# Projection of the merged sum: one fp32 product or three fp32r products

## The chip, the cores and the metric

One Trainium2 chip, of which the kernel uses one core. Its engines run side by side: PE (TensorE, matrix products, its results go to the PSUM banks), DVE (VectorE), ACT (ScalarE), POOL (GpSimd) and SP (SyncE), which here issues nearly all transfers from HBM. The metric is the device time of one execution in microseconds (us); lower is better.

## The reference, cut to what matters

The program is a chain of two transformer-like blocks over 256 tokens of width 1024: gated linear attention, product-key retrieval, sliding-window attention, retrieval again, then a mixer of retention and latent attention, and a routed mixture of experts. Everything is in fp32. The change is in the mixer's last two lines:

```python
def token_mixer(...):
    ...
    y_ret = (jax.nn.silu(rg) * y_ret) @ w_ret_o
    y_mla = mla(...) @ w_mla_o
    merged = jax.nn.sigmoid(gate_ret) * y_ret + jax.nn.sigmoid(gate_mla) * y_mla
    return merged @ w_out            # (256, 1024) @ (1024, 1024)
...
h = h + g1 * token_mixer(...)
u = modulate_2(rmsnorm_2(h, norm2[l]), sh2, sc2)
h = h + g2 * hier_moe(u, ...)        # router, top 2 of 32 experts, three products each
```

## The kernel before, in words

Activations are kept with features on the partitions: a tensor of width 1024 is eight chunks of 128 features by T = 256 tokens. A projection makes one output chunk at a time, in one of four PSUM banks that are used in turn. Its weights come as slots of 128 x 1024 values (512 KB) through a ring of four slots (`ring`). SP issues the load of a slot when PE has begun the chunk three before it (`ring_free`).

There are two ways to make a product of an input and a slot. `project` (L871) multiplies in fp32: eight products of 128x128 by 128x256 for a chunk, each recorded as two instructions. `project_split` (L814) splits both operands into a high part, rounded to fp32r, and a low part, the rest, and adds three fp32r products (high by high, high by low, low by high): 24 instructions for a chunk. For that the weights of a slot are split in two halves of 512 columns. ACT writes the high part (`split_high`, L1529: it waits for the slot's landing, and for `x_passed`, by which PE tells that it has begun the half three before, so that one of the four buffers `w_parts` is free). DVE writes the low part by a subtraction (`split_lows`, L2026) and signals `x_low`, for which PE waits. The list `SPLIT` (L91) names the slots that go this way and numbers their halves. The inputs' parts lie in `h_parts`.

Around the change the order is this. PE runs the eight chunks of `mla_o` (tiles `m_out0` to `m_out7`) split. ACT makes the high parts two chunks ahead, DVE the low parts. When a chunk is full, DVE multiplies it by the gate `M.gm` into SBUF (L2674), adds `M.gr` (L2676) and signals `merged`. Then PE runs the eight chunks of `mix_out` (tiles `mix0` to `mix7`) in fp32 from `M.mg` (`project_norm`, L1330). Behind each, DVE adds the result into the residual `xT` (`update_dve`, L2034), ACT squares it (`squares_act`, L1512), and from the third chunk on PE adds up a chunk of squares with a matrix of ones (L770). After chunks 3 and 5, ACT also makes high parts of the first expert's weights (`experts_high`), and POOL their low parts (`moe_pool`, L2899, four instructions at L2903).

Then comes the root of the norm: ACT writes a logarithm and an exponential of the sum of squares, DVE the mean (L1951) and three steps of refinement in `root_dve` (L1959, L1961, L1963), then eight scalings (L1976) that ACT shifts (L1576). Meanwhile PE multiplies five times by the unit matrix for nothing (`keep_clock`, L866), and then begins the router's product (L1352), each step of which waits for a shifted chunk. The routing and the experts follow.

SP's queue there: the loads of `mix_out` 0 to 3, then, once `merged` is 1, two of 1 MB for the first expert (L707), then `mix_out` 4 to 7 and the router.

Of the kernel before, what the change touches and what calls it, by code (L numbers as in the profile page):

```python
# [39 lines left out]
P = 128  # L40
D = 1024
T = 256
# [51 lines left out]
          ("gate_r", 0, 8), ("gate_m", 0, 8), ("mla_o", 0, 8)) for k in range(first, last)]  # L94
# [116 lines left out]
def block_program(nc, stream, vecs, xin, pos, wg2, subk, consts, consts_g, consts_s, consts2, consts_e, out):  # L211
    ctx = ExitStack()
    with ctx:
# [232 lines left out]
        M.mg = M.g  # L446
# [341 lines left out]
        def project_split_norm(pe, name, tile, u, parts):  # L788

            for c in range(DC):  # L790
                project_split(pe, name, c, f"{tile}{c}", parts if c == 0 else None)
                if c >= 2:
                    square_sum_pe(pe, u, c - 2)
            for c in (DC - 2, DC - 1):
                square_sum_pe(pe, u, c)
# [18 lines left out]
        def project_split(pe, name, k, tile, parts=None):  # L814
# [3 lines left out]
            for j in range(2):  # L818
# [4 lines left out]
                for q in range(4):  # L823
                    for i, (wp, hp) in enumerate(((0, 0), (0, 1), (1, 0))):
                        mm = pe.matmul(t[:, 0:T], w[:, wp, q * P:(q + 1) * P], h_parts[:, hp, 4 * j + q, :],  # L825
                                       start=(j == 0 and q == 0 and i == 0), stop=(j == 1 and q == 3 and i == 2))
                        if j == 0 and q == 0 and i == 0:
                            mm.then_inc(ring_free, 1)
                        if q == 0 and i == 1:

                            mm.then_inc(sem("x_passed"), 1)
# [375 lines left out]
        def mix_pe(pe):  # L1207
# [122 lines left out]
            project_norm(pe, "mix_out", M.mg, "mix", "2b", lambda q: (sem("merged"), q + 1))  # L1330
# [438 lines left out]
        def mix_act(act):  # L1769
# [73 lines left out]
            for c in range(2, DC):  # L1843
                for j in range(2):
                    split_high(act, "mla_o", c, j)
# [55 lines left out]
        def _(act):  # L1901
# [39 lines left out]
            squares_act(act, "2b", "mix", highs={3: 0, 5: 1})  # L1941
# [622 lines left out]
        def mix_dve(dve):  # L2564
# [104 lines left out]
            for c in range(DC):  # L2669
                if c + 2 < DC:  # L2670
                    split_lows(dve, "mla_o", c + 2)
                dve.wait_ge(full_sem(f"m_out{c}"), filled(f"m_out{c}"))
                t = tile_of(f"m_out{c}")
                dve.tensor_tensor(M.gm[:, c, :], t[:, 0:T], M.gm[:, c, :], ALU.mult).then_inc(free_sem(f"m_out{c}"), 1)  # L2674
                dve.wait_ge(free_sem(f"m_out{c}"), freed(f"m_out{c}"))
                dve.tensor_tensor(M.mg[:, c, :], M.gr[:, c, :], M.gm[:, c, :], ALU.add).then_inc(sem("merged"), 1)  # L2676
# [264 lines left out]

        def mods_pool(pool, seg, c):
# [6 lines left out]
        def _(pool):  # L2949
# [4 lines left out]
            peer_pool(pool, 1)  # L2954
            moe_pool(pool)
# [136 lines left out]
```

## Time and profile before

| | us |
|---|---|
| median of three runs | 2817.7 (2816.72 to 2817.91) |
| the profiled execution | 2811.54 |
| its span | 2809.4 |
| busy in the span: PE, DVE, ACT, POOL | 2724.4, 2133.0, 1322.8, 1284.3 |
| mean granted clock | 0.983 of full speed |

The span is from the first to the last instruction; the execution is 2.1 us longer. All times in the rows are us from the start of the span, except where ns is written. In a timeline, instructions of one kind that follow each other are merged into one row with their count (x...), and the bracket at its end says how long the engine was idle before and whose signal ended that. Matmuls overlap, so the durations of single ones add up to more than the distance between their starts. PEclk is the share of the full clock that TensorE was granted.

### The profile page before, as it was taken

To read this page: it belongs to the slowest core of one execution; us is meant where nothing else is said; L and a number is where in the kernel's file an instruction comes from. 1 tells how busy PE (TensorE), PEld (TensorE's weight loads), DVE (VectorE), ACT (ScalarE), POOL (GpSimd) and SP (SyncE) were. 2 spreads that over 40 slices of the span, in tenths; PEclk is the share of its full clock that TensorE was granted. 3 is DMA by queue.
4 is the path that set the end of the run, shared out by engine and by line. 5 is a ranking of instruction groups with operands and counts; after the bars stand their busy time and mean duration, and the time that the engine had idled before them with its cause. 6 is when DMAs were issued, how large, how long until landed. Compare 5 with 4: busy or idle time off the path is not lost.

```text
span 2809.4 us, 53370 instructions
## 1 busy us (share of the span) xinstructions
PE 2724.4 (97%) x16610; PEld 2396.3 (85%) x16610; DVE 2133.0 (76%) x4130; ACT 1322.8 (47%) x2530; POOL 1284.3 (46%) x973
## 2 busy tenths in 40 slices
PE   6999999999999999899999999999999999999998
PEld 6688999999878887799999998788878998776665
DVE  7735996999888886758967898888867544477876
ACT  1115555333455555555564434555555643254553
POOL 4940897666454441005987664544430000154442
PEclk8999999999999999899999999999999999999999
DMA  7634555666666663144554466766644533399994
GB/s 258 217 113 137 179 180 194 203 204 202 228 247 226 238 237 114 56 137 150 181 182 138 166 202 205 263 227 228 233 148 165 181 129 121 116 360 356 356 356 174
DMA packets 179366, 562.52 MB, mean 200 GB/s; under 512 B 16288, under 2 KB 19104, under 8 KB 179120
## 3 DMA queue, kind: packets, MB, share of 16 engines
q1 hardware_dynamic: 176880, 556.86, 57.1%
q10 hardware_dynamic: 2368, 4.19, 0.5%
q8 instruction: 61, 1.00, 0.1%
q14 instruction: 57, 0.47, 0.1%
HBM read 559.94 MB, written 1.05 MB: 200 GB/s over the span
## 4 chain that ended last, share of the span: by engine, by line
PE 78%; PEld 6%; issue 6%; DVE 4%; POOL 2%; ACT 2%; DMA 1%; ACTq 0%; DVEq 0%; PEldq 0%; SPq 0%; POOLq 0%
PE bank L1112 23%; PE bank L1081 20%; PE bank L825 8%; PE bank L1417 7%; PEld bank L1081 6%; PE bank L1061 4%; PE bank L1438 4%; PE bank L884 4%; PE bank L849 1%; POOL arena L2928 1%; PE bank L770 1%; POOL arena L2930 1%; ACT arena L1728 1%; PE bank L1251 1%; DVE a_parts L2460 1%
## 5 line engine op out<-in xcount | busy, mean ns | idle before, releaser
L2880 POOL TENSOR_TENSOR w_parts<-ring,w_parts 128x512 fp32r<-128x512 f32 x512 | 665.3, 1306 | 514.5 <-ACT w_parts L1645 479.8
L1081 PE MATMUL bank<-h_parts,w_parts 128*128 128x256 f32 x6144 | 771.4, 285 | 4.5 <-POOL w_parts L2880 2.3
L1081 PEld LDWEIGHTS bank<-h_parts,w_parts 128*128 128x128 f32 x6144 | 747.5, 192 | 4.8 <-POOL w_parts L2880 2.4
L1645 ACT ACTIVATE w_parts<-ring 128x512 fp32r<-128x512 f32 x512 | 322.8, 631 | 436.5 <-PE bank L1081 435.9
L1112 PE MATMUL bank<-w_parts,a_parts 128*128 128x512 f32 x1536 | 370.3, 397 | 3.5 <-DVE a_parts L2460 3.5
L1112 PE MATMUL bank<-h_parts,a_parts 128*128 128x512 f32 x1536 | 364.1, 392 | 4.4 <-DVE a_parts L2460 4.1
L1112 PEld LDWEIGHTS bank<-h_parts,a_parts 128*128 128x128 f32 x1536 | 285.2, 188 | 75.5 <-DVE a_parts L2460 17.0
L1112 PEld LDWEIGHTS bank<-w_parts,a_parts 128*128 128x128 f32 x1536 | 285.9, 190 | 63.0 <-DVE a_parts L2460 4.5
L825 PE MATMUL bank<-h_parts,w_parts 128*128 128x256 f32 x2304 | 283.4, 285 | 4.1 <-DVE w_parts L2031 4.1
L825 PEld LDWEIGHTS bank<-h_parts,w_parts 128*128 128x128 f32 x2304 | 280.6, 193 | 5.1 <-issue 4.4
L1703 ACT ACTIVATE a_parts<-arena 128x256 fp32r (+1 forms) x256 | 107.0, 418 | 355.7 <-PE bank L1112 355.7
L2460 DVE TENSOR_TENSOR a_parts<-arena,a_parts 128x256 fp32r<-128x256 f32 x256 | 166.0, 649 | 116.4 <-ACT a_parts L1703 115.8
L2031 DVE TENSOR_TENSOR w_parts<-ring,w_parts 128x512 fp32r<-128x512 f32 x216 | 147.3, 691 | 120.6 <-ACT w_parts L1535 119.4
L2819 DVE TENSOR_TENSOR e_parts<-arena,e_parts 128x1024 fp32r<-128x1024 f32 x136 | 183.2, 1388 | 71.5 <-ACT e_parts L1510 71.3
L2402 DVE TENSOR_SCALAR hT<-bank,mean 128x128 f32<-128x128 f32 x512 | 200.7, 402 | 22.8 <-PEq L1041 22.8
L1417 PE MATMUL bank<-e_parts,h_parts 128*128 128x512 f32 x816 | 214.2, 412 | 0.0
L1417 PEld LDWEIGHTS bank<-e_parts,h_parts 128*128 128x128 f32 x816 | 150.8, 188 | 45.2 <-issue 15.5
L1510 ACT ACTIVATE e_parts<-arena 128x1024 fp32r<-128x1024 f32 x140 | 140.4, 1052 | 91.1 <-DMA arena<-stream 91.1
L1535 ACT ACTIVATE w_parts<-ring 128x512 fp32r<-128x512 f32 x216 | 134.9, 630 | 84.6 <-PE bank L825 59.7
L2903 POOL TENSOR_TENSOR e_parts<-arena,e_parts 128x1024 fp32r<-128x1024 f32 x4 | 9.3, 2355 | 338.5 <-ACT e_parts L1510 338.5
L1581 ACT ACTIVATE arena<-bank 128x256 f32<-128x256 f32 (+2 forms) x205 | 84.8, 414 | 164.4 <-PE bank L884 55.7
L2457 DVE TENSOR_TENSOR h_parts<-ring,h_parts 128x512 fp32r<-128x512 f32 x144 | 156.7, 1128 | 0.6
(399 smaller groups left out, 4257.2 us busy)
## 6 DMA issues: line engine op xcount, KB each, us to landing
ring<-stream SPq DMA_DIRECT2D x594, 512.0 KB, 3.3
arena<-stream SPq DMA_DIRECT2D x105, 1024.0 KB, 7.4
arena<-stream SPq DMA_DIRECT2D x144, 512.0 KB, 4.5
hT<-stream SPq DMA_DIRECT2D x96, 256.0 KB, 3.1
hT<-stream SPq DMA_DIRECT2D x32, 512.0 KB, 4.8
mean<-stream SPq DMA_DIRECT2D x32, 512.0 KB, 4.6
arena<-consts ACTq DMA_DIRECT2D x1, 1536.0 KB, 6.4
xT<-xin ACTq DMA_DIRECT2D x1, 1024.0 KB, 10.6
```

Of the source, the lines that this page charges most:

```text
L825: mm = pe.matmul(t[:, 0:T], w[:, wp, q * P:(q + 1) * P], h_parts[:, hp, 4 * j + q, :], start=(j == 0 and q == 0 and i == 0), stop=(j == 1 ...
L1081: mm = pe.matmul(bank[k][:, 0:T], w[:, wp, ws], h_parts[:, hp, 4 * j + q, :], start=(j == 0 and q == 0 and i == 0), stop=(j == 1 and q == ...
L1112: mm = pe.matmul(bank[4 + 2 * a + e][:, :], a_parts[:, k % 2, ap, a * P:(a + 1) * P], w[:, wp, :], start=False, stop=False, skip_group_che ...
L1417: mm = pe.matmul(o, step_x(p, x, 4 * h + q), E.hl[u % PARTED][:, wp, :, q * P:(q + 1) * P], start=(h == 0 and q == 0 and i == 0), stop=(h ...
L1510: act.activation(E.hl[u % PARTED][:, 0, s, :], E.raw[:, u % RAWS, s, :], ACT.Copy).then_inc(sem("e_high"), 1)
L1645: act.activation(w_parts[half % HALVES][:, 0, :], ring[slot_][:, j * 512:(j + 1) * 512], ACT.Copy).then_inc(sem(f"{n}_high"), 1)
L2031: dve.tensor_tensor(w[:, 1, :], slot(name, k)[:, j * 512:(j + 1) * 512], w[:, 0, :].bitcast(F32), ALU.subtract).then_inc(sem("x_low"), 1)
L2402: dve.tensor_scalar(hot1[:, GROUP * (k % 2) + s, :], iota_p, route[:, 0, bass.ds(at + s, 1)], route[:, 2, bass.ds(at + s, 1)], ALU.is_equa ...
L2457: dve.tensor_tensor(w[:, 1, :], v_slot(l, k)[:, j * 512:(j + 1) * 512], w[:, 0, :].bitcast(F32), ALU.subtract).then_inc(sem(f"{n}_low"), 1)
L2460: dve.tensor_tensor(a_parts[:, k % 2, 1, :], W[:, bass.ds(it * 16 + k, 1), :].rearrange("p i t -> p (i t)"), a_parts[:, k % 2, 0, :].bitca ...
L2819: ins = dve.tensor_tensor(E.hl[u % PARTED][:, 1, s, :], E.raw[:, u % RAWS, s, :], E.hl[u % PARTED][:, 0, s, :].bitcast(F32), ALU.subtract)
L2880: pool.tensor_tensor(w[:, 1, :], ring[(base + k) % RING][:, j * 512:(j + 1) * 512], w[:, 0, :].bitcast(F32), ALU.subtract).then_inc(sem(f" ...
```

## The change

The slots of `mix_out` join the list `SPLIT`, and their chunks run through `project_split`, with the new tile `M.mg_parts` (high and low part of the merged sum) in the place of `h_parts`. Each product of input chunk q waits for `mg_low` >= q + 1.

The merge of a chunk is written in PSUM: DVE multiplies the bank by `M.gm` in place, adds `M.gr` in place and signals `merged`; ACT copies it to the high part; DVE subtracts this from the bank for the low part, and only then gives the bank back. ACT's splitting of weights goes on through `mla_o` 2 to 7 and `mix_out` 0 and 1, one chunk behind each merge, and for `mix_out` 2 to 7 in `squares_act`. The low parts of these weights (`mla_o` 2 to 7 and `mix_out` 0 to 7) move from DVE to POOL, in front of `moe_pool`.

```diff
-          ("gate_r", 0, 8), ("gate_m", 0, 8), ("mla_o", 0, 8)) for k in range(first, last)]
+          ("gate_r", 0, 8), ("gate_m", 0, 8), ("mla_o", 0, 8), ("mix_out", 0, 8)) for k in range(first, last)]
...
-        M.mg = M.g
+        M.mg_parts = rounded("m_mg_parts", 4 * CH, 4 * CH).rearrange("p (x c t) -> p x c t", x=2, c=8)
...
-        def project_split(pe, name, k, tile, parts=None):
+        def project_split(pe, name, k, tile, parts=None, src=h_parts, made=None):
...
                 for q in range(4):
+                    if made is not None:
+                        pe.wait_ge(sem(made), 4 * j + q + 1)
                     for i, (wp, hp) in enumerate(((0, 0), (0, 1), (1, 0))):
-                        mm = pe.matmul(t[:, 0:T], w[:, wp, q * P:(q + 1) * P], h_parts[:, hp, 4 * j + q, :],
+                        mm = pe.matmul(t[:, 0:T], w[:, wp, q * P:(q + 1) * P], src[:, hp, 4 * j + q, :],
...
-            project_norm(pe, "mix_out", M.mg, "mix", "2b", lambda q: (sem("merged"), q + 1))
+            project_split_norm(pe, "mix_out", "mix", "2b", None, M.mg_parts, "mg_low")
...
-            for c in range(2, DC):
+            for c in range(DC):
                 for j in range(2):
-                    split_high(act, "mla_o", c, j)
+                    split_high(act, *(("mla_o", c + 2) if c + 2 < DC else ("mix_out", c + 2 - DC)), j)
+                act.wait_ge(sem("merged"), c + 1)
+                act.activation(M.mg_parts[:, 0, c, :], tile_of(f"m_out{c}")[:, 0:T], ACT.Copy).then_inc(sem("mg_high"), 1)
...
-            squares_act(act, "2b", "mix", highs={3: 0, 5: 1})
+            squares_act(act, "2b", "mix", "mix_out", highs={3: 0, 5: 1})
...
             for c in range(DC):
-                if c + 2 < DC:
-                    split_lows(dve, "mla_o", c + 2)
                 dve.wait_ge(full_sem(f"m_out{c}"), filled(f"m_out{c}"))
-                t = tile_of(f"m_out{c}")
-                dve.tensor_tensor(M.gm[:, c, :], t[:, 0:T], M.gm[:, c, :], ALU.mult).then_inc(free_sem(f"m_out{c}"), 1)
+                t = tile_of(f"m_out{c}")[:, 0:T]
+                dve.tensor_tensor(t, t, M.gm[:, c, :], ALU.mult).then_inc(signal("dve_step"), 1)
+                dve.wait_ge(sem("dve_step"), signalled("dve_step"))
+                dve.tensor_tensor(t, t, M.gr[:, c, :], ALU.add).then_inc(sem("merged"), 1)
+                dve.wait_ge(sem("mg_high"), c + 1)
+                dve.tensor_tensor(M.mg_parts[:, 1, c, :], t, M.mg_parts[:, 0, c, :].bitcast(F32), ALU.subtract)\
+                   .then_inc(free_sem(f"m_out{c}"), 1)
                 dve.wait_ge(free_sem(f"m_out{c}"), freed(f"m_out{c}"))
-                dve.tensor_tensor(M.mg[:, c, :], M.gr[:, c, :], M.gm[:, c, :], ALU.add).then_inc(sem("merged"), 1)
+                dve.sem_inc(sem("mg_low"), 1)
...
+        def split_lows_pool(pool, name, k):
+            for j in range(2):
+                half = split_half(name, k, j)
+                w = split_parts(name, k, j)
+                pool.wait_ge(sem("x_low"), half)
+                pool.wait_ge(sem("x_high"), half + 1)
+                pool.tensor_tensor(w[:, 1, :], slot(name, k)[:, j * 512:(j + 1) * 512], w[:, 0, :].bitcast(F32),
+                                   ALU.subtract).then_inc(sem("x_low"), 1)
...
             peer_pool(pool, 1)
+            for name, first in (("mla_o", 2), ("mix_out", 0)):
+                for k in range(first, DC):
+                    split_lows_pool(pool, name, k)
             moe_pool(pool)
```

On POOL, behind the second retrieval, before:

```order
L2940 TENSOR_TENSOR hT<-mean 128x128
L2894 REGISTER_ALU
L2894 COMPARE_AND_BRANCH
L2903 TENSOR_TENSOR e_parts_52<-arena,e_parts_52 128x1024 x2
L2903 TENSOR_TENSOR e_parts_53<-arena,e_parts_53 128x1024 x2
L2906 MEMSET ring 128x4096
```

and of the changed kernel (`e_parts` are the parts of the experts' weights; the numbers of these buffers went up by one with the new tile):

```order
L2947 TENSOR_TENSOR hT<-mean 128x128
L2901 REGISTER_ALU
L2901 COMPARE_AND_BRANCH
L2956 TENSOR_TENSOR w_parts<-ring,w_parts 128x512 x28
L2910 TENSOR_TENSOR e_parts_53<-arena,e_parts_53 128x1024 x2
L2910 TENSOR_TENSOR e_parts_54<-arena,e_parts_54 128x1024 x2
L2913 MEMSET ring 128x4096
```

The 28 low parts stand in front of the four subtractions for the first expert, in one queue.

On ACT, from the loading of the logarithm's table to the shifts of the norm, before:

```order
L1501 ACT_TABLE_LOAD
L1521 ACTIVATE hT<-xT 128x256 x4
L1510 ACTIVATE e_parts_52<-arena 128x1024 x2
L1521 ACTIVATE hT<-xT 128x256 x2
L1510 ACTIVATE e_parts_53<-arena 128x1024 x2
L1521 ACTIVATE hT<-xT 128x256 x2
```

and the first part of the same stretch of the changed kernel (L1537 is a high part of `mix_out`, L1523 a square, L1512 the experts' high parts):

```order
L1503 ACT_TABLE_LOAD
L1537 ACTIVATE w_parts<-ring 128x512 x2
L1523 ACTIVATE hT<-xT 128x256
L1537 ACTIVATE w_parts<-ring 128x512 x2
L1523 ACTIVATE hT<-xT 128x256
L1537 ACTIVATE w_parts<-ring 128x512 x2
L1523 ACTIVATE hT<-xT 128x256
L1537 ACTIVATE w_parts<-ring 128x512 x2
L1523 ACTIVATE hT<-xT 128x256
L1512 ACTIVATE e_parts_53<-arena 128x1024 x2
```

Each square stands behind the two high parts of the chunk two further on.

## Rows read from the trace of the kernel before

**Rows 1.** The page: first lines of parts 1 and 4 (busy time, chain).
```profile
PE 2724.4 (97%) x16610; PEld 2396.3 (85%) x16610; DVE 2133.0 (76%) x4130; ACT 1322.8 (47%) x2530; POOL 1284.3 (46%) x973
...
PE 78%; PEld 6%; issue 6%; DVE 4%; POOL 2%; ACT 2%; DMA 1%; ACTq 0%; DVEq 0%; PEldq 0%; SPq 0%; POOLq 0%
```

**Rows 2.** Timeline of PE, 2373 to 2443 us; columns: start us, us, engine, line, operation.
```profile
2373.93 23.27 PE L825 MATMUL bank<-h_parts,w_parts 128*128 128x256 f32 x192
2397.04 10.52 PE L884 MATMUL bank<-arena,ring 128*128 128x256 f32 x48
...
2423.37 3.62 PE L884 MATMUL bank<-arena,ring 128*128 128x256 f32 x16
2426.82 1.03 PE L770 MATMUL bank<-hT,cst 128*128 128x256 f32 x4
...
2428.61 2.32 PE L869 MATMUL bank<-cst 128*128 128x256 f32 x10
2432.41 3.62 PE L1352 MATMUL bank<-hT,ring 128*36 128x256 f32 x16 [1.47 <-ACT hT L1576]
...
2442.20 0.89 PE L1361 MATMUL bank<-cst,hT 128*128 128x128 f32 x4 [4.01 <-DVE h_parts L2744]
```

**Rows 3.** Timeline of ACT, 2377 to 2394 us.
```profile
2377.38 0.63 ACT L1535 ACTIVATE w_parts<-ring 128x512 fp32r<-128x512 f32 x1 [0.81 <-PE bank L825]
...
2392.43 1.28 ACT L1501 ACT_TABLE_LOAD   x1
```

**Rows 4.** Timeline of DVE, 2397 to 2432 us.
```profile
2397.24 0.42 DVE L2674 TENSOR_TENSOR arena<-bank,arena 128x256 f32<-128x256 f32 x1 [1.99 <-PE bank L825]
...
2423.20 0.48 DVE L2039 SCALAR_TENSOR_TENSOR xT<-bank,modv,xT 128x256 f32<-128x256 f32 x1 [3.40 <-PE bank L884]
...
2429.85 0.43 DVE L1959 TENSOR_TENSOR hT<-rs 128x256 f32<-128x256 f32 x1
...
2431.24 3.22 DVE L1976 SCALAR_TENSOR_TENSOR hT<-xT,gain,bank 128x256 f32<-128x256 f32 x8
```

**Rows 5.** Timeline of POOL in the first retrieval, from 399.8 us.
```profile
399.81 16.37 POOL L2880 TENSOR_TENSOR w_parts<-ring,w_parts 128x512 fp32r<-128x512 f32 x12 [0.91 <-ACT w_parts L1645]
```

**Rows 6.** Timeline of POOL: its last work before the routing.
```profile
2421.28 4.67 POOL L2903 TENSOR_TENSOR e_parts<-arena,e_parts 128x1024 fp32r<-128x1024 f32 x2 [3.11 <-ACT e_parts L1510]
```

**Rows 7.** Timeline of SP's queue of transfers, 2397 to 2416 us.
```profile
2398.04 0.98 SPq L707 DMA_DIRECT2D arena<-stream  x2
2401.11 11.55 SPq L622 DMA_DIRECT2D ring<-stream  x4
```

**Rows 8.** Transfers issued in 2400 to 2402 us: count, KB each, us to landing.
```profile
ring<-stream SPq DMA_DIRECT2D x1, 512.0 KB, 7.4
```

**Rows 9.** Timeline of DVE, 26 to 29 us: the root of the first norm.
```profile
26.42 1.11 DVE L1959 TENSOR_TENSOR hT<-rs 128x256 f32<-128x256 f32 x1
27.56 0.83 DVE L1961 SCALAR_TENSOR_TENSOR hT<-hT,mean 128x256 f32<-128x256 f32 x1
28.42 0.57 DVE L1963 SCALAR_TENSOR_TENSOR bank<-hT,rs 128x256 f32<-128x256 f32 x1
```

**Rows 10.** Timeline of POOL in the same stretch.
```profile
25.98 1.26 POOL L2930 TENSOR_TENSOR arena<-arena 128x512 f32<-128x512 f32 x1
27.32 0.78 POOL L2932 TENSOR_TENSOR arena<-arena 128x256 f32<-128x256 f32 x1
28.18 0.51 POOL L2940 TENSOR_TENSOR arena<-arena 128x128 f32<-128x128 f32 x1
```

**Rows 11.** Timeline of DVE from 409 us, while POOL makes low parts.
```profile
409.84 0.70 DVE L2363 TENSOR_TENSOR bank<-bank,arena 128x512 f32<-128x512 f32 x1
```

**Rows 12.** Timeline of PE from 2123 us, after an idle gap.
```profile
2123.10 12.08 PE L825 MATMUL bank<-h_parts,w_parts 128*128 128x256 f32 x79 [4.05 <-DVE w_parts L2031]
```

**Rows 13.** Busy time by stage, 2441 to 2446.7 us; after POOL: granted clock, DMA, GB/s.
```profile
2441.00:2442.20 1.20, 0.00 (x0) 0.00 (x0) 1.11 (x4) 0.00 (x0) 0.00 (x0) 1.00 0.00 0
...
2443.20:2443.70 0.50, 0.50 (x2) 0.36 (x2) 0.00 (x0) 0.50 (x2) 0.00 (x0) 0.50 0.76 270
```

More of the change, by code:

```diff
@@ L786, in project_norm, with project_split_norm @@
                 square_sum_pe(pe, u, c)
-        def project_split_norm(pe, name, tile, u, parts):
+        def project_split_norm(pe, name, tile, u, parts=None, src=h_parts, made=None):
             for c in range(DC):
-                project_split(pe, name, c, f"{tile}{c}", parts if c == 0 else None)
+                project_split(pe, name, c, f"{tile}{c}", parts if c == 0 else None, src, made if c == 0 else None)
                 if c >= 2:
```

## The prediction

> **What bounds the kernel now.** I read the page first. PE is busy nearly all of the span and holds 78% of the chain that ended last [rows 1], so time is won or lost only where PE's own work gets shorter or where PE comes to wait. Then the timeline of PE at the place of the change [rows 2]. The reader is to see three things in it. The eight split chunks of `mla_o` take from 2373.93 to 2397.04, 23.11 us for 192 products: 0.1204 each, 2.89 a chunk. The fp32 chunks of `mix_out` take 3.45 each (2423.37 to 2426.82), and the five sums of squares between them make up the rest of 2397.04 to 2426.82: (29.78 - 27.60) / 5 = 0.44 each. No row from 2373.93 to 2426.82 has a bracket, so PE never waits there. Behind it PE waits for the norm: the idle multiplications end at 2428.61 + 2.32 = 2430.93, and the router starts at 2432.41. There the path goes through ACT's and DVE's root and the scalings at 2431.24 [rows 4]. So a shortening of `mix_out` is on the path, but what follows must come as much earlier, and that hangs on DVE.
>
> All times below are on this execution: 2811.54 us, a span of 2809.4 and 2.1 around it. It lies 6.2 below the median of 2817.7; I work out a difference and add it to the median.
>
> **PE's products.** Out go 8 x 3.45 = 27.6 us, in come 8 x 2.89 = 23.1 us: -4.5. The same form on the same shapes stands directly in front in the trace, so I take the 2.89 as it is.
>
> **The merge.** DVE's product with a PSUM source takes 0.42 [rows 4]; the sum (0.42 as well) and the subtraction have the same size. With ACT's copy of a 128x256 bank, which I put at 0.42 too, a chunk's chain is 4 x 0.42 and four signals of some 0.05: 1.9 us, below PE's 2.89 a chunk. The last chunk is full at 2397.2; its parts are there by 2399.2 to 2399.3, since ACT is still at a high part (0.63 [rows 3]) when the sum is ready. PE wants them for the eighth input chunk of `mix0`, 21 products after 2397.04: 2399.57. Cost 0, with 0.3 to spare; without that cover it is the difference, at most 0.5. On ACT the load of the table (1.28 [rows 3]), which before lay in an idle stretch, now comes after the last merge, at 2398.7, and delays `mix_out` 2's high parts to 2400.0; PE wants that chunk at 2402.8, and 0.63 + 1.36 fit. Cost 0.
>
> **The low parts on POOL.** Twelve lows of this form in a row took 16.37 us, 1.364 each [rows 5], of which 1.31 are the instruction. PE takes 1.44 a half. So POOL keeps up, but makes good only 0.08 a half once it is behind. A high and a low (0.63 + 1.31 + 0.1 of signals = 2.0) fit into the three halves (4.3) by which ACT may run ahead. Cost 0 where the weights are there in time. DVE's released time is worth nothing: it idled there.
>
> **The load of `mix_out` 4.** SP issues it when PE begins `mix1`, behind two loads of 1 MB of 2398.04; it was issued at 2401.11 and landed 7.4 later, at 2408.5 [rows 7, 8]. In fp32 PE needed it only at 2411.7. Now PE wants it split at 2397.04 + 4 x 2.89 + 2 x 0.44 = 2409.5. The issue comes 0.5 earlier, but the two large loads ahead stay where they are, so it lands at 2408.0 to 2408.5; the first half is split 2.0 later, at 2410.0 to 2410.5. Cost 0.5 to 1.0. From below it could be 0 (it lands as fast after its issue as a load without such neighbours), from above 2 (`mix_out` 5 is issued 1.1 earlier and shares the queue with it). I take 1.0, nearest to the row. PE then reaches the end of `mix7` at 2426.82 - 4.5 + 1.0, 3.5 earlier than before.
>
> **POOL behind the lows.** This is the term that the diff does not show. From `mix_out` 4's landing POOL runs back to back: its first low starts at 2408.5 + 0.7 = 2409.2, eight lows of 1.364 end at 2420.1. Only then come the four subtractions for the first expert, which before ended at 2421.28 + 4.67 = 2425.95, ahead of the root of the norm at 2429.85 [rows 4, 6]. At 2.34 each they now end at 2422.5, 2424.8, 2427.2 and 2429.5. The root moves to 2429.85 - 3.5 = 2426.35, into the third of them.
>
> What that does is to be read at the first norm, where POOL was at work too: the three steps took 1.11, 0.83 and 0.57 instead of 0.43, and ended at 27.53, 28.39 and 28.99, each 0.29 to 0.30 after the end of the POOL instruction that ran beside it (27.24, 28.10, 28.69) [rows 9, 10]. All three read two operands from SBUF. A DVE instruction with one operand in PSUM was not held up: 0.70 for 128x512 while POOL made lows, 0.48 for the residual's update while POOL worked at the experts' lows [rows 4, 5, 11]. So the merge and the updates are safe (by that), and the first two steps of the root are not: the first ends at 2427.2 + 0.3 = 2427.5, the second at 2429.5 + 0.3 = 2429.8, the third at 2430.25, and the scalings, one operand of which is in PSUM, start at 2430.3. Undisturbed they would at 2431.24 - 3.5 = 2427.7. Cost 2.6. Its bounds: 0, if POOL's instruction gives way to DVE's, and 3.0, if POOL's lows run some tenths later.
>
> The Trainium skill has a rule on this, in "SBUF — State Buffer", section "Who interferes with whom": a DVE instruction with two SBUF inputs contends with a GpSimd instruction that reads SBUF, and whichever was issued first holds the shared port to its end. The rows agree on both kinds (1.11 against 0.43, and 0.70 with PSUM). It also says that DVE wins if it comes first; by that the cost would be 0 where the root falls between two POOL instructions, but POOL leaves no such gap here.
>
> **The clock.** The router's first product then starts 0.9 earlier than before, at 2431.5, but the idle multiplications end 3.5 earlier, at 2427.4. PE idles 4.1 us there instead of 1.47. After its two idle gaps of this length in the trace (4.05 and 4.01 [rows 2, 12]) the granted clock was half, 1.2 GHz: 0.50 at 2443.2 [rows 13], and the 79 products from 2123.10 took 12.08 instead of 79 x 0.1204 = 9.5, which is 2.6 lost. The router's 16 instructions (3.5 us) are about half as long as that stretch, and the norm's shifts feed them at full speed. At half clock throughout they would lose 3.5, at the row's loss 2.6, at full clock 0. I take 1.9, since part of them can be late anyhow behind ACT's shifts. Behind the routing everything is released by what the routing gives, and moves as it does.
>
> **Sum.** -4.5 + 1.0 + 2.6 + 1.9 = +1.0: 2817.7 + 1.0 = 2818.7 (2812.5 for a profiled execution like this one).
>
> **The rivals.**
> - *B, the clock holds.* The root is held up, but PE's 4.1 us idle do not cost the clock. For it: only two gaps of this length are seen, and they were of 4.0 us, so a somewhat shorter one may be spared. Against: both fell. -4.5 + 1.0 + 2.6 = -0.9: 2816.8.
> - *C, DVE and POOL do not meet.* The lows run ahead, or the root slips in first. For it: the rows on POOL are of other operands and lengths. Against: four subtractions need 9.4 us behind the last low, and `mix7` with the update, the square and the logarithm only 6 to 7; no shift of a few tenths parts them. The clock holds then too. -4.5 + 1.0 = -3.5: 2814.2, and with `mix_out` 4 in time 2813.2. That is the change as it reads.
> - *D, slower: the merge is held up by POOL.* If an in-place operation on PSUM with one SBUF input does queue behind POOL's lows, each of the three DVE operations of a chunk waits for one: 3 x 1.36 + 0.5 = 4.6 a chunk instead of 2.89, and seven chunks behind the first put the last 7 x 1.7 = 12 us late. 2818.7 + 12 = 2830.7. It decides from the point at which a chunk's chain is longer than 2.89. Against it stand the 0.70 and 0.48 above.
>
> The first norm's rows speak for the forecast most directly, so I give it 50%, B 22%, C 17%, D 4%, and 7% to something that none of them names.
>
> **How the numbers follow.** What a measurement of this kernel can tell from no change is about 0.2%, 5.6 us. Neither the forecast, B nor C reaches it: even the whole -4.5 is 0.16%. Slower by over 0.2% is D and the far end of the forecast (`mix_out` 4 at 2.0, root at 3.0, clock at 3.5: +4.0, with something unnamed): 7%. Faster by over 0.2% needs something unnamed: 5%. Within: 88%. The range takes in the forecast, B and most of C below, and the bounds of the unknown costs above: 2813.5 to 2821.5.
>
> **What would show it.** Each `mix` chunk at 2.89 on PE; one wait of PE of about 1 us at `mix4`, for POOL's low part; POOL's four subtractions in one run behind the lows, over the root; the steps of L1959 and L1961 at 1 to 2 us each, L1963 at 0.43; DVE's merge operations at 0.42; PE idle for about 4 us before the router, and the clock at half in it. The forecast is wrong if the root's steps take 0.43 with POOL at work beside them, if `mix4` starts later than 2412, or if the merge operations are longer than 0.5.

## The result, and the profile after

The changed kernel takes 2819.05 us (median of 12 runs, 2815.82 to 2825.53); the kernel before, beside it, 2815.47 (2811.66 to 2817.91). The ratio is 1.0017, 95% interval [1.0009, 1.0025]: 4.8 us more, 2.5 to 7.0 (the two medians lie 3.6 apart). The predicted time was 2818.7, in a range of 2813.5 to 2821.5. The time lies in the range, but the forecast's difference was +1.0, and that is too small. The ratios of the experiments leave out two executions that lie far from all others, 3853.87 us (both_mended, the one that was profiled) and 8625.81 us (loads_apart).

The two profiled executions can't be compared at their ends. The first product of `mla_o`, ahead of which both programs are the same, starts at 2373.93 before and at 2378.54 after, 4.6 us apart; over all profiles of this study it starts between 2370.3 and 2382.8. So I count from this product, M below. The column "routed" is the time from the product that turns the router's logits to the first product that gathers tokens for the experts.

| us from M | before | after | difference |
|---|---|---|---|
| last sum of squares | 54.15 | 51.12 | -3.03 |
| router starts | 58.48 | 58.01 | -0.47 |
| logits turned | 62.61 | 63.83 | +1.22 |
| first gather | 76.81 | 80.64 | +3.83 |
| routed | 14.20 | 16.81 | +2.61 |

Timeline of PE after, in answer to [rows 2]:

```profile
2401.65 8.80 PE L827 MATMUL bank<-m_mg_parts,w_parts 128*128 128x256 f32 x72
...
2413.59 0.59 PE L770 MATMUL bank<-hT,cst 128*128 128x256 f32 x2
2415.56 3.11 PE L827 MATMUL bank<-m_mg_parts,w_parts 128*128 128x256 f32 x24 [1.38 <-POOL w_parts L2956]
...
2430.20 2.32 PE L871 MATMUL bank<-cst 128*128 128x256 f32 x10
2436.55 5.30 PE L1354 MATMUL bank<-hT,ring 128*36 128x256 f32 x16 [4.03 <-ACT hT L1578]
...
2448.03 1.12 PE L1363 MATMUL bank<-cst,hT 128*128 128x128 f32 x4 [4.00 <-DVE h_parts L2751]
```

The reader is to see the three chunks in 8.80, one wait at `mix4`, 4.03 idle ahead of the router instead of 1.47, and the router's 16 instructions in 5.30 instead of 3.62. POOL's timeline, in answer to [rows 6], and DVE's, in answer to [rows 4]:

```profile
2414.14 10.97 POOL L2956 TENSOR_TENSOR w_parts<-ring,w_parts 128x512 fp32r<-128x512 f32 x8 [3.42 <-ACT w_parts L1537]
2425.08 9.53 POOL L2910 TENSOR_TENSOR e_parts<-arena,e_parts 128x1024 fp32r<-128x1024 f32 x4
```

```profile
2402.32 0.43 DVE L2678 TENSOR_TENSOR bank<-bank,arena 128x256 f32<-128x256 f32 x1
...
2431.44 0.97 DVE L1963 TENSOR_TENSOR hT<-rs 128x256 f32<-128x256 f32 x1
2432.44 2.44 DVE L1965 SCALAR_TENSOR_TENSOR hT<-hT,mean 128x256 f32<-128x256 f32 x1
2434.92 0.43 DVE L1967 SCALAR_TENSOR_TENSOR bank<-hT,rs 128x256 f32<-128x256 f32 x1
2435.39 3.22 DVE L1980 SCALAR_TENSOR_TENSOR hT<-xT,gain,bank 128x256 f32<-128x256 f32 x8
```

POOL is busy without a break from 2414.14 to 2434.61. The second step of the root ends at 2434.88, 0.27 after POOL; the third, which follows POOL's end, takes its 0.43. Clock in stretches (columns: stretch, length, busy PE, PEld, DVE, ACT, POOL; then granted clock, DMA share, GB/s), in answer to [rows 13], after and then before:

```profile
2437.50:2439.50 2.00, 2.00 (x6) 0.90 (x5) 1.13 (x4) 1.70 (x5) 0.00 (x0) 0.50 0.00 0
2439.50:2441.50 2.00, 2.00 (x9) 0.92 (x7) 0.00 (x0) 0.00 (x0) 0.00 (x0) 0.80 0.00 0
2448.00:2452.00 4.00, 3.97 (x14) 3.44 (x14) 0.69 (x1) 0.91 (x3) 0.00 (x0) 0.50 0.82 262
2452.00:2456.00 4.00, 4.00 (x14) 3.55 (x15) 2.11 (x8) 0.00 (x0) 0.00 (x0) 0.50 0.00 0
```

```profile
2444.00:2446.00 2.00, 2.00 (x8) 1.64 (x7) 0.00 (x0) 0.07 (x1) 0.00 (x0) 0.52 0.91 375
2446.00:2448.00 2.00, 2.00 (x14) 1.87 (x14) 0.99 (x5) 0.00 (x0) 0.00 (x0) 1.00 0.00 0
```

The last two rows of the first fence and both rows of the second are of the routing. Its gap is 4.0 us in both kernels, but PE's clock was at half (1.2 GHz) from 2442.5 to 2445.9 before, 3.4 us, and from 2447.1 to 2457.4 after, 10.2 us. That is the row which the prediction lacks.

### The profile page after: what moved, and what is told of

It is laid out like the page before. It is cut to its first block and busy times, and to the rows that moved or that the text cites. A ratio compares the mean times of both kernels' runs of the same rounds, so it can differ in the third digit from the quotient of the medians.

```text
span 2819.0 us, 53599 instructions
## 1 busy us (share of the span) xinstructions
PE 2731.4 (97%) x16674; PEld 2400.1 (85%) x16674; DVE 2146.4 (76%) x4126; ACT 1335.6 (47%) x2554; POOL 1328.2 (47%) x1001
## 3 DMA queue, kind: packets, MB, share of 16 engines
q10 hardware_dynamic: 2368, 4.19, 0.4%
## 5 line engine op out<-in xcount | busy, mean ns | idle before, releaser
L2887 POOL TENSOR_TENSOR w_parts<-ring,w_parts 128x512 fp32r<-128x512 f32 x512 | 667.8, 1311 | 509.5 <-ACT w_parts L1647 476.3
L1647 ACT ACTIVATE w_parts<-ring 128x512 fp32r<-128x512 f32 x512 | 322.8, 631 | 436.2 <-PE bank L1083 435.7
L2035 DVE TENSOR_TENSOR w_parts<-ring,w_parts 128x512 fp32r<-128x512 f32 x204 | 139.0, 691 | 114.6 <-ACT w_parts L1537 113.2
L1537 ACT ACTIVATE w_parts<-ring 128x512 fp32r<-128x512 f32 x232 | 144.8, 630 | 92.6 <-PE bank L827 64.5
L1512 ACT ACTIVATE e_parts<-arena 128x1024 fp32r<-128x1024 f32 x140 | 140.4, 1051 | 96.3 <-DMA arena<-stream 96.3
L2956 POOL TENSOR_TENSOR w_parts<-ring,w_parts 128x512 fp32r<-128x512 f32 x28 | 36.7, 1309 | 305.7 <-ACT w_parts L1537 302.8
```

The lines of the kernel that those rows point to most:

```text
L1512: act.activation(E.hl[u % PARTED][:, 0, s, :], E.raw[:, u % RAWS, s, :], ACT.Copy).then_inc(sem("e_high"), 1)
L1537: act.activation(split_parts(name, k, j)[:, 0, :], slot(name, k)[:, j * 512:(j + 1) * 512], ACT.Copy).then_inc(sem("x_high"), 1)
L1647: act.activation(w_parts[half % HALVES][:, 0, :], ring[slot_][:, j * 512:(j + 1) * 512], ACT.Copy).then_inc(sem(f"{n}_high"), 1)
L2887: pool.tensor_tensor(w[:, 1, :], ring[(base + k) % RING][:, j * 512:(j + 1) * 512], w[:, 0, :].bitcast(F32), ALU.subtract).then_inc(sem(f" ...
```

## The experiments

Twelve kernels ran, in three groups of four, each timed beside the kernel before. My theory after the result was that of the forecast: POOL's low parts over the root, and the clock behind the idle gap that this makes. A ratio is to the kernel before of the same group.

| | ratio, interval | last squares | router | routed | gather |
|---|---|---|---|---|---|
| before | | 54.15 | 58.48 | 14.20 | 76.81 |
| after | 1.0017 [1.0009, 1.0025] | 51.12 | 58.01 | 16.81 | 80.64 |
| pool_after_root | 1.0006 [0.9996, 1.0016] | 51.15 | 55.48 | 16.90 | 76.51 |
| idle_filled | 1.0004 [0.9995, 1.0013] | 51.38 | 58.24 | 14.19 | 76.56 |
| loads_apart | 1.0001 [0.9991, 1.0011] | 49.50 | 56.55 | 14.03 | 77.30 |
| both_mended | 0.9997 [0.9984, 1.0009] | | | | |
| before_pool_late | 1.0031 [1.0021, 1.0041] | 54.15 | 61.69 | 16.67 | 84.18 |
| before_pool_lows | 0.9994 [0.9982, 1.0005] | 54.15 | 58.48 | 14.20 | 76.81 |
| lows_on_dve | 1.0011 [1.0002, 1.0019] | 52.50 | 58.97 | 14.19 | 77.29 |
| gap_filled_too | 0.9989 [0.9977, 1.0001] | 49.52 | 53.84 | 15.07 | 73.04 |
| d1_root_in_psum | 0.9995 [0.9984, 1.0006] | 51.13 | 55.77 | 13.95 | 73.85 |
| d2_root_psum_apart | 0.9985 [0.9974, 0.9996] | 49.50 | 54.14 | 14.67 | 72.94 |
| d4_psum_apart_filled | 0.9976 [0.9962, 0.9989] | 49.51 | 54.14 | 12.53 | 70.80 |
| d3_before_gap_filled | 0.9992 [0.9982, 1.0003] | 54.16 | 58.48 | 12.53 | 75.14 |

The stages are of one profile each, in us from M; both_mended has times alone. With two exceptions, lows_on_dve (+0.5 at the gather, 3.1 by the ratio) and pool_after_root (-0.3, 1.7), the shift of the gather and the ratio agree within 1.8 us. The stretch from the gather to the end took 358.6 to 362.1 in every profile, with no order in it by kernel.

**pool_after_root.** POOL's work for the experts waits until the root is done.

```diff
 def moe_pool(pool):
+    pool.wait_ge(sem("norm_scaled"), scaled("2b", 0))
```

> The changed kernel, but POOL waits for the first scaling of the norm before it makes the low parts of the first expert's weights, so that none of them lies over the root. Theory (the root is held up behind POOL, PE idles 4 us, the clock falls): the root's three steps take 0.43 each, 2.6 us less together; PE's idle gap before the router is 1.9 us or less instead of 4.03; the router's 16 instructions take 3.6 us instead of 5.3. The time is 4.3 us below the changed kernel's. POOL's four subtractions end some 10 us after the root, before PE wants them. Rival (the lost gain is in the split projection, or it is run to run scatter elsewhere): root and router move, but the time stays within 1.5 us of the changed kernel's.

The three steps took 0.42, 0.42 and 0.43, and the router ran at full clock, 2.5 us earlier than in the changed kernel. But POOL's four subtractions now ran from 2425.19 to 2434.48, over the routing, and DVE's small steps there met them:

```profile
2425.19 9.29 POOL L2911 TENSOR_TENSOR e_parts<-arena,e_parts 128x1024 fp32r<-128x1024 f32 x4 [8.27 <-DVE hT L1980]
```

```profile
2430.94 1.28 DVE L2693 COPY arena<-arena 128x8 f32<-128x8 f32 x1
2432.25 0.24 DVE L2699 MAX8 arena<-arena 128x8 f32<-128x8 f32 x2
...
2432.93 1.59 DVE L2706 CAST arena<-arena 128x16 f32<-128x16 uint32 x1
```

```profile
2438.10 1.11 PE L1363 MATMUL bank<-cst,hT 128*128 128x128 f32 x4 [6.52 <-DVE h_parts L2751]
```

In the changed kernel these two took 0.17 each and PE's gap was 4.00, so the 2.5 that the root gave was lost again there. (That "routed" is nevertheless as long as in the changed kernel is due to the clock, which was at half for 3.9 us behind this gap, and for 9.3 behind the gap there.) By the ratios the kernel is 3.1 us faster than the changed one, where I had expected 4.3. The root's part is shown; the remedy only moves the collision.

**idle_filled.** Thirteen idle multiplications by the unit matrix instead of five, so that PE does not stand still ahead of the router.

```diff
 def moe_pe(pe):
-    keep_clock(pe, 5)
+    keep_clock(pe, 13)
```

> The changed kernel with 13 instead of 5 idle multiplications of PE before the router (8 more, 3.5 us), so that PE's gap there is about 0.6 us; the root stays held up. Theory: the steps of the root still take 0.97 and 2.44, the router starts at the same distance from the merge as in the changed kernel, but at full clock, and takes 3.6 us instead of 5.3: 1.7 us less, and perhaps more behind it. Rival (the router was slow for another cause than the clock): it still takes 5.3 us.

```profile
2436.14 3.62 PE L1354 MATMUL bank<-hT,ring 128*36 128x256 f32 x16 [0.54 <-ACT hT L1578]
```

The root was held up as in the changed kernel (0.92 and 2.46), PE idled 0.54, and the router took 3.62 at a clock of 1.00, from 58.24: the logits were turned at 62.37 instead of 63.83. So 1.5 to 1.7 us of the router's loss is the clock alone. The routing, which the edit does not touch, took 14.19 instead of 16.81, with the same gap of 4.00 and the clock at half for 3.4 us only. So the gather came 4.1 earlier than in the changed kernel, and by the ratios the time is 3.7 us lower.

**loads_apart.** The second 1 MB load for the first expert goes behind `mix_out` 5.

```diff
-for u in range(2):
-    up_load(u, slice(SO["moe"][0], SO["moe"][0] + 4))
-loads(MO["mix_out"][0] + RING, MO["mix_out"][1])
+up_load(0, slice(SO["moe"][0], SO["moe"][0] + 4))
+for k in range(RING, 8):
+    load(MO["mix_out"][0] + k)
+    if k == RING + 1:
+        up_load(1, slice(SO["moe"][0], SO["moe"][0] + 4))
```

> The changed kernel, but of the two 1 MB loads for the first expert the second is issued behind the load of mix_out chunk 5 instead of ahead of chunk 4's. Theory (chunk 4 is late because it queues behind 2 MB): it lands some 6 us after its issue instead of 8.5, and PE's wait of 1.38 us at mix4 is gone; since POOL and the root still meet, little of it reaches the end: 0 to 1.4 us less. Rival (POOL is too slow for the half): the wait at mix4 or another of 1 us stays.

Transfers issued with `mix_out` 4's load, after, and then in this kernel (count, KB, us to landing):

```profile
ring<-stream SPq DMA_DIRECT2D x1, 512.0 KB, 8.5
```

```profile
ring<-stream SPq DMA_DIRECT2D x1, 512.0 KB, 5.2
```

The wait at `mix4` is gone, and the last sum of squares comes 1.6 earlier. The root still fell under POOL's subtractions, and the router took 6.21 us:

```profile
2433.23 6.21 PE L1356 MATMUL bank<-hT,ring 128*36 128x256 f32 x16 [4.19 <-ACT hT L1580]
2433.00:2439.00 6.00, 5.77 (x15) 2.62 (x16) 2.31 (x7) 2.88 (x8) 0.00 (x0) 0.54 0.00 0
```

The clock was 0.54 in it. Of the 1.6, 0.56 is left when the logits are turned (63.27 against 63.83). The routing took 14.03 here with two gaps of 4 us as in the changed kernel; that speaks against a fixed price of the second gap. By the ratios the kernel is 4.5 us faster than the changed one, more than the 0 to 1.4 that I had expected; the gather came 3.3 earlier, and 2.8 of that is the shorter routing, not the load.

**both_mended** has the last edit and that of pool_after_root together.

> The changed kernel with both: POOL's experts' lows behind the root, and the two 1 MB loads apart. Theory: no wait in the split projection, root undisturbed, clock held: from the first product of mla_o to the router's first 4.5 us less than before the change (54.0 instead of 58.5), and a time 4.5 us below the kernel before, 5 to 8 below the changed one. Rival: what is won is given back in the routing behind it, where PE's next gap of 4 us lies: under 2 us below the kernel before.

I had expected 4.5 us below the kernel before. The ratio, 0.9997, is 0.8 below, from 4.5 below to 2.5 above; it does not part this kernel from the kernel before or from either of its halves, and it does not decide between the theory and its rival. Inconclusive.

**before_pool_late.** The mirror: in the kernel before, POOL's work for the first expert waits for the seventh square.

```diff
 def moe_pool(pool):
+    pool.wait_ge(sem("norm_squares"), squared("2b", 6))
```

> The kernel before, unchanged but for POOL: it waits for the seventh square of the norm before it makes the four low parts of the first expert's weights, so that they lie over the root. Nothing is split that was not. Theory: the root's first two steps are each held to the end of one of POOL's instructions (up to 2.4 us each, 2 to 4 us together), the router starts that much later with PE idle 3.5 us or more, and the clock is half in the router: 3 to 6 us slower than the kernel before. Rival (the root does not depend on POOL): the steps take 0.43 and the time is the same.

```profile
2427.11 9.45 POOL L2904 TENSOR_TENSOR e_parts<-arena,e_parts 128x1024 fp32r<-128x1024 f32 x4 [344.34 <-ACT hT L1521]
```

```profile
2432.74 1.62 DVE L1959 TENSOR_TENSOR hT<-rs 128x256 f32<-128x256 f32 x1
2434.40 2.44 DVE L1961 SCALAR_TENSOR_TENSOR hT<-hT,mean 128x256 f32<-128x256 f32 x1
2436.87 0.43 DVE L1963 SCALAR_TENSOR_TENSOR bank<-hT,rs 128x256 f32<-128x256 f32 x1
```

The same steps are held up with nothing else of the change present: 4.68 idle, router 3.2 later, gather 7.4 later, 8.7 us by the ratio, more than the 3 to 6 that I had expected: here too the routing took 2.5 longer than before (16.67), which I had not counted. POOL's place is shown to be enough to lose more than the whole gain of PE's products.

**before_pool_lows.** In the kernel before, POOL alone makes the low parts of `mla_o` 2 to 7 (the twelve that `split_lows` made on DVE).

> The kernel before with one part of the change alone: POOL makes the low parts of mla_o chunks 2 to 7, mix_out stays in fp32 and the merge in SBUF. Theory: the time is the same within 1 us, since DVE idled there and POOL keeps up; but the merge's sum, which reads two operands from SBUF, takes up to 1.3 us instead of 0.42 where a POOL instruction runs beside it, while the product, with one in PSUM, stays at 0.42. Rival (keeping the merge in PSUM is not what spares it): both take 0.42.

```profile
2377.86 17.15 POOL L2947 TENSOR_TENSOR w_parts<-ring,w_parts 128x512 fp32r<-128x512 f32 x12 [296.89 <-ACT w_parts L1535]
```

```profile
2381.10 0.42 DVE L2672 TENSOR_TENSOR arena<-bank,arena 128x256 f32<-128x256 f32 x1 [1.66 <-PE bank L825]
2381.56 0.77 DVE L2674 TENSOR_TENSOR arena<-arena 128x256 f32<-128x256 f32 x1
```

Two operations of one length, 128x256, back to back, with POOL busy beside both: the one with a PSUM operand takes its 0.42, the one with two in SBUF 0.77. So it is in six of the eight chunks; in the last two, behind POOL's end at 2395.01, both take 0.42. There is slack for it, and every stage stands where it stood. Moving these lows costs nothing; what costs is the queue behind those of `mix_out`.

**lows_on_dve.** The changed kernel with all low parts of the weights back on DVE, woven between the merge and the updates.

```diff
+                of = ("mla_o", c + 2) if c + 2 < DC else ("mix_out", c + 2 - DC)
+                split_lows(dve, *of, (0,))
                 dve.wait_ge(sem("mg_high"), c + 1)
...
+                split_lows(dve, *of, (1,))
-            update_dve(dve, "mix", mod(112 + 16))
+            for c in range(DC):
+                if c + 2 < DC:
+                    split_lows(dve, "mix_out", c + 2)
+                update_dve(dve, "mix", mod(112 + 16), (c,))
...
-            for name, first in (("mla_o", 2), ("mix_out", 0)):
-                for k in range(first, DC):
-                    split_lows_pool(pool, name, k)
```

> The changed kernel, but DVE makes the low parts of mla_o 2 to 7 and of mix_out, and POOL none. DVE then has 2 x 0.69 + 3 x 0.43 = 2.7 us a chunk in 2.89. Theory: the projection runs as in the changed kernel (wait at mix4 shorter, since DVE's low takes 0.69 instead of 1.31); POOL's experts' lows start when ACT has their high parts and end before the root; so the root is undisturbed and the router at full clock: 4 to 5 us below the changed kernel. Rival (DVE has no room for it): PE waits in each chunk, and the time is at or above the changed kernel's.

```profile
2421.18 1.30 DVE L2035 TENSOR_TENSOR w_parts<-ring,w_parts 128x512 fp32r<-128x512 f32 x2 [1.07 <-ACT w_parts L1537]
...
2425.84 4.23 DVE L2035 TENSOR_TENSOR w_parts<-ring,w_parts 128x512 fp32r<-128x512 f32 x2 [2.97 <-ACT w_parts L1537]
...
2438.36 1.31 DVE L1963 TENSOR_TENSOR hT<-rs 128x256 f32<-128x256 f32 x1
```

That expectation failed. POOL's own four subtractions (2424.35, 2434.71) stayed, and DVE's low parts, with two operands in SBUF, now met them: 4.23 for two instead of 1.30. PE waited 1.34 and 1.04 for them, and the root's first step took 1.31. (A wait of 0.78 at `mix4` came earlier, when POOL was idle; it was 1.38 in the changed kernel.) The ratio is 1.0011, 1.7 us below the changed kernel's instead of 4 to 5. With the work on either engine the two collide; only the victim changes.

**gap_filled_too.** both_mended, and eight more idle multiplications in the gap of the routing.

```diff
-            for i in range(1, 4):
-                slots_turned(i)
+            for i in range(1, 3):
+                slots_turned(i)
+            keep_clock(pe, 8)
+            slots_turned(3)
             keep_clock(pe, 3)
```

> The changed kernel with POOL's experts' lows behind the root, the loads apart, and 8 idle multiplications of PE in its gap of 4.0 us in the routing, ahead of the last turning of the slots. Theory (a gap of 4 us costs the clock there too, in the kernel before and after): granted clock 1.0 from there to the gathering of the slots, which starts 2 to 5 us earlier than in both_mended; time 6 to 9 us below the kernel before. Rival (DVE sets the pace there and not PE): the clock is full, but the time is as both_mended's.

The clock stayed at 1.00 from the router to the gather, the gap that is left is 3.10 since DVE was held up as in pool_after_root (1.29 and 1.60), and the gather comes 3.8 before that of the kernel before. The ratio, 0.9989, is 3.1 us below the kernel before, half or less of the 6 to 9 that I had expected, and its interval just reaches 1.

**d1_root_in_psum.** Instead of moving POOL, DVE's three steps get an operand in PSUM each. That asks for a second exponential on ACT.

```diff
-            root_act(act, "2b", rs[:, :])
...
+            act.activation(bank[5][:, 0:T], rs[:, :], ACT.Exp, scale=-0.5)
+            act.activation(rs[:, :], rs[:, :], ACT.Exp, scale=-0.5).then_inc(sem("norm_root"), 1)
...
+                r, r_bank, t = rs[:, :], bank[5][:, 0:T], bank[5][:, T:2 * T]
...
+                dve.tensor_tensor(t, r, r_bank, ALU.mult).then_inc(signal("dve_step"), 1)
...
+                dve.scalar_tensor_tensor(t, t, -0.5, mean[:, 0, :], ALU.mult, ALU.mult).then_inc(signal("dve_step"), 1)
...
+                dve.scalar_tensor_tensor(root, t, 1.5, r, ALU.add, ALU.mult).then_inc(signal("dve_step"), 1)
```

The exponential `r` lies in SBUF and, as `r_bank`, in PSUM; the intermediate `t`, which the changed kernel keeps in SBUF, is in PSUM.

> The changed kernel, but the root of the norm is kept partly in a PSUM bank: ACT writes the exponential twice (bank 5 and SBUF, 0.4 us more), and each of DVE's three steps then has one operand in PSUM; POOL's low parts stay where they are, over the root. Theory (an instruction of DVE with two SBUF operands waits for POOL's, one with a PSUM operand does not): the steps take 0.42 to 0.48 each with POOL's subtractions beside them; the router starts about 2 us earlier than in the changed kernel relative to the first product of mla_o (55.9 instead of 58.0), with about 2 us idle before it and at full clock (3.6 us); the routing starts as early as POOL's low parts allow, so DVE's small routing steps are partly held up; the gather comes 2 to 4 us earlier than in the changed kernel (77 to 79 instead of 80.6), the time is 2 to 4 us below it, within 0.1% of the kernel before. Rival (it is the engine DVE that is slowed by POOL's work, whatever the operands): the first two steps stay at 1.0 and 2.4 us, and the time is that of the changed kernel or 0.4 more.

Timelines of POOL and DVE of this kernel:

```profile
2425.90 9.35 POOL L2924 TENSOR_TENSOR e_parts<-arena,e_parts 128x1024 fp32r<-128x1024 f32 x4
```

```profile
2432.57 0.43 DVE L1981 TENSOR_TENSOR bank<-rs,bank 128x256 f32<-128x256 f32 x1 [0.33 <-ACT rs L1950]
2433.03 0.43 DVE L1983 SCALAR_TENSOR_TENSOR bank<-bank,mean 128x256 f32<-128x256 f32 x1
2433.50 0.43 DVE L1985 SCALAR_TENSOR_TENSOR bank<-bank,rs 128x256 f32<-128x256 f32 x1
```

POOL works from 2425.90 to 2435.25, over all three steps, and none is longer by it. This is the run that parts the theories: the operands decide, not POOL's work as such. The router came at 55.77 at full clock. The gather, at 73.85, came 3 to 5 us earlier than I had expected, because POOL is done at 2435.25 and the routing's steps begin at 2440.01: there is nothing left to collide. By the ratios the kernel is 6.2 us faster than the changed one, more than the expected 2 to 4. The second exponential costs 0.31 of idle time (1.78 against 1.47).

**d2_root_psum_apart** adds the loads of loads_apart.

> As d1_root_in_psum, and the first expert's second load of 1 MB is issued behind mix_out 5 instead of ahead of mix_out 4. Theory: mix4's load is there in time, so the last square sum comes 1.5 us earlier (49.5), the router starts at 54 to 54.5 with under 2.5 us idle before it; the gather at 75 to 77; the time 3 to 5 us below the changed kernel, 0 to 2 us below the one before. Rival (what is gained ahead of the routing is lost again in it, since POOL's low parts end at a fixed time and hold up DVE's routing steps): the gather stays at 78 or more and the time is that of d1.

Last squares 49.50, router 54.14, gather 72.94: 2.1 us earlier than I had expected at the least. The ratio is 0.9985 [0.9974, 0.9996], 4.2 us below the kernel before instead of 0 to 2, and this is the first variant whose interval lies below 1.

**d4_psum_apart_filled** adds the filled gap of gap_filled_too.

> As d2_root_psum_apart, with eight more multiplications by the unit matrix in PE's gap during the routing (they give nothing to the result). Theory (each idle gap of about 4 us costs half the clock behind it): PE holds the full clock through the routing, and the gather comes at 71 to 74, the earliest of all variants; 4 to 6 us below the kernel before, ratio 0.998 to 0.9985. Rival (the later stages do not follow, since they are bound by loads that are issued by other events): the gather comes earlier, but the stretch from the gather to the end becomes longer by as much, and the ratio is 1.000.

```profile
2437.06 0.66 PE L1365 MATMUL bank<-cst,hT 128*128 128x128 f32 x4 [0.55 <-DVE h_parts L2769]
```

```profile
2437.00:2440.00 3.00, 2.94 (x21) 2.79 (x22) 0.69 (x2) 0.91 (x3) 0.00 (x0) 1.00 0.84 259
2440.00:2444.00 4.00, 4.00 (x20) 3.28 (x19) 3.71 (x11) 0.00 (x0) 0.00 (x0) 1.00 0.17 68
```

The gap is 0.55, the clock 1.00 behind it, the gather at 70.80, 6.0 us ahead of the kernel before. Median 2805.78 us (9 runs, 2804.49 to 2811.3), ratio 0.9976 [0.9962, 0.9989]: 6.8 us below before, somewhat more than the expected 4 to 6, and the fastest version found (its interval overlaps that of d2_root_psum_apart). The rival, a longer way from the gather on, does not hold (358.78 against 358.66).

**d3_before_gap_filled** is the kernel before with that filled gap alone.

> The kernel before, with the eight more multiplications by the unit matrix in PE's gap during the routing. Theory: the clock stays at full behind the gap, where it was at half for some 3 us; the gather comes 1.5 to 2.5 us earlier (74.3 to 75.3 instead of 76.8 after the first product of mla_o), and the time is 1.5 to 2.5 us lower, 0.9991 to 0.9995. Rival (the products there are paced by DVE and ACT and do not need the clock): the gather stays at 76.8 and the time is the same.

The gather came at 75.14, 1.67 earlier, as expected. The ratio, 0.9992 [0.9982, 1.0003], has the expected size but does not part it from no change.

## Why the prediction was right, and where its sum was not

- **PE's products, -4.5.** Right: three chunks in 8.80, and with the load's term the last squares come 3.03 earlier, where -4.5 + 1.38 gives -3.1.
- **The merge, 0.** Right: 0.43, 0.43 and 0.42, with POOL at work beside most of them, and no bracket on PE before `mix4`. D did not happen.
- **Low parts on POOL, 0.** Right; before_pool_lows shows it alone.
- **`mix_out` 4's load, +1.0.** Somewhat small: PE waited 1.38. The load was issued 0.9 earlier after M but took 8.5 instead of 7.4 [rows 8], so it landed 0.2 later. loads_apart shows that the 1 MB load ahead of it is the cause.
- **Root behind POOL, +2.6.** Right, down to the instruction: the first step ran into the third of POOL's four subtractions, the second into the fourth, and the scalings start 56.85 after M, in pool_after_root 54.31: 2.54. C, in which the two do not meet, is out; d1_root_in_psum shows the mechanism.
- **Clock in the router, +1.9.** Right: 4.03 idle (4.1 predicted), and from the router's start to the turned logits 5.82 instead of 4.13, 1.69 more. idle_filled takes it away. B is out. That the size fits is in part luck: 1.9 was a choice between 0 and 3.5, and in loads_apart the same loss, behind a gap of 4.19, was 2.59 (6.72 against 4.13).
- **The routing, 0.** This step failed. The sum has no term for the routing: it passes from the router's clock to "Behind the routing everything is released by what the routing gives, and moves as it does", and gives no reason why the routing itself should take as long as before. The sum up to the logits was +1.22, where +1.0 was forecast; the routing then took 2.61 longer, because the half clock behind its 4.00 gap lasted 10.2 us instead of 3.4. That brings +3.83 at the gather, and the measured 4.8 (2.5 to 7.0) fits it; +1.0 lies outside, and so does +1.22. From the gather on the quoted sentence holds: 359.8 us to the end against 358.7, inside the spread of all profiles.
- **The base.** That the predicted time was hit is in part luck: I added to a median of three runs, 2817.7, which the twelve beside the changed kernel put at 2815.47. On that base the forecast is 2816.5, 2.6 below the measured median.
- **What can be told from no change.** I put it at 0.2%. The interval of the ratio came out narrower, 0.08% to either side, so that a difference of 0.17% stands clear of none.

What stays open is why the half clock lasts longer in some profiles. Behind the routing's gap it lasted 10.2 us in two of the three profiles that have another gap of 4 us or more ahead of the router (after, before_pool_late), and 3.4 in the third (loads_apart). In the profiles with the routing's gap alone and at 4.0 us it lasted 3.4, but 6.8 in d2_root_psum_apart, and the routing took 13.95 to 14.67; pool_after_root's 16.90 is its longer gap of 6.52. One profile of each can't settle whether the first gap causes it.

Chance has a part in it, and the traces show that at places which no edit touches. Behind PE's gap of 4.05 ahead of M [rows 12] the half clock lasted 6.8 us in ten of the thirteen profiles and 3.4 in three (pool_after_root, lows_on_dve, gap_filled_too). Behind an earlier gap of 2.98 to 2.99 the clock fell in eleven profiles and not at all in two (pool_after_root, before_pool_late). In the kernel before it fell there:

```profile
1180.76 0.80 PE L1160 MATMUL bank<-arena 128*128 128x128 f32 x2 [2.98 <-ACT arena L1581]
1182.00:1184.00 2.00, 2.00 (x11) 2.00 (x11) 1.93 (x10) 0.87 (x2) 0.00 (x0) 0.50 0.00 0
```

So the 2.61 of one profile could be an accident of that execution. Against this stands the ratio of twelve runs, whose interval has room for +3.83 and not for +1.22; that supports a longer routing in most executions of the changed kernel, and does not show it.

## What to carry to other kernels

Work moved to POOL lengthens POOL's queue for whatever stands behind it. Look for where that later work now runs, and which DVE instructions with two operands in SBUF lie beside it on the path. Giving such an instruction one operand in PSUM cures it where moving POOL's work only moves the collision (gather at 76.51 in pool_after_root, at 73.85 in d1_root_in_psum; their ratios, 1.0006 and 0.9995, have intervals that overlap). And an idle gap of PE can have a price of its own behind it, which differs from execution to execution: read the clock after every gap of the new kernel, the old ones too, before a time is summed.

## What the runs showed of the hardware

- A DVE instruction with two operands in SBUF that met POOL's work ended when POOL's instruction had: 0.97 and 2.44 instead of 0.43 each (after). With one operand in PSUM it took 0.43 beside the same work (d1_root_in_psum).
- POOL holds up more than two-operand arithmetic. With POOL at work (pool_after_root), a COPY of 128x8 took 1.28 and a CAST of 128x16 1.59 instead of 0.17 each, though each reads one operand; MAX8 and FIND_INDEX8 beside them kept 0.24 and 0.16. The Trainium skill says so in "SBUF — State Buffer", section "Who interferes with whom": copies and casts may enter a mode that takes the pair of ports shared with GpSimd. The rows agree.
- From M to the gather, the granted clock was half behind each gap of 4.00 us and more, and full behind those of 3.10 (gap_filled_too), 2.35 (lows_on_dve), 1.78 and 1.47. That is no limit: elsewhere a gap of 2.98 was followed by half clock (before), and the same gap of 2.99 was not (pool_after_root). How long it stayed at half differed between executions for gaps of one length: 3.4 us before, 10.2 after, for 4.01 and 4.00.
- A 512 KB load took 5.2 us to land with one 1 MB load ahead of it (loads_apart), and 7.4 and 8.5 with two (before, after).
- Eight idle multiplications in a gap in which PE has nothing to do took 1.67 us off the routing (d3_before_gap_filled; clock 1.00 behind it instead of 0.50).
